# Tables of a state space layer made in the first stage, its work in other slots, and one root for the norm of all heads

## The reference

```python
z = rmsnorm(x, g_mix) @ w_in
q, k, v, u = split(z)                                # 1024 columns each
attn = diff_attend(rope(q), rope(k), v, ...)         # 8 heads; the 8 decoding tokens attend to 2048 cached ones each
o = o * rsqrt(mean(o * o, axis=-1) + EPS)            # norm of each head, over its 128 values
o = o * g_sub * (1.0 - lam_init)

# state space layer: 64 groups of 16 channels, 64 complex states each
dt = exp(log_dt); mag = exp(a_re * dt)
lr, li = mag * cos(a_im * dt), mag * sin(a_im * dt)
bbar = (lam - 1) / a * b                             # complex
h[t] = lam * h[t-1] + bbar @ u[t];  y = Re(c @ h) + d * u
y = gelu(y); y = y * sigmoid(y @ w_glu + b_glu)

x = x + concat(attn, y) @ w_out
x = x + peer(rmsnorm(x, g_ffn), ...)                 # product-key experts
y = rmsnorm(x, g_final)
```

## Time and profile before

| | |
|---|---|
| median of 3 runs | 3755.88 us (3750.92 to 3758.41) |
| profiled execution | 3757.6 us, its span 3755.8 |
| mean granted PE clock | 0.973 |
| busy: PE, DVE, ACT, POOL | 94%, 55%, 29%, 52% |
| HBM | 236 GB/s over the span |

### The profile page before, as it was taken

One profiled execution on the slowest core, in us unless ns is written; L12 is line 12 of the kernel. 1 busy time (PEld: TensorE's weight loads), 2 busy tenths in 40 slices (PEclk: granted clock), 3 DMA queues, 4 the chain that ended last, 5 costly groups with the idle time before them and its releaser, 6 DMA issues. The chain is left out here.

```text
span 3755.8 us, 57507 instructions
## 1 busy us (share of the span) xinstructions
PE 3526.1 (94%) x22816; PEld 3336.9 (89%) x22816; DVE 2071.7 (55%) x3748; ACT 1079.7 (29%) x1184; POOL 1944.8 (52%) x735
## 2 busy tenths in 40 slices
PE   8999966887997999999999999997999999999997
PEld 8988743556997999999999999997999999999997
DVE  4212076426103899974444444443677777767673
ACT  3111132235122222333333333332222222222222
POOL 3333217004434445666666566654766667767662
PEclk9999978898998999999999999998999999999999
DMA  5587676562321225777777777767877878778772
GB/s 217 197 298 289 238 209 222 183 233 108 115 110 73 79 98 180 281 272 275 276 290 274 275 276 289 285 265 277 299 280 289 303 291 295 288 296 296 294 286 102
DMA packets 252324, 892.41 MB, mean 238 GB/s; under 512 B 97873, under 2 KB 131154, under 8 KB 175058
## 3 DMA queue, kind: packets, MB, share of 16 engines
q1 hardware_dynamic: 168882, 548.78, 41.1%
q0 software_dynamic: 36864, 268.45, 17.5%
q10 hardware_dynamic: 46432, 73.32, 5.7%
HBM read 818.91 MB, written 69.21 MB: 236 GB/s over the span
## 5 line engine op out<-in xcount | busy, mean ns | idle before, releaser
L113 POOL TENSOR_TENSOR wl<-raw,wh 128x2048 fp32r<-128x2048 f32 x324 | 1525.0, 4707 | 1559.0 <-ACT wh L109 1558.9
L109 ACT ACTIVATE wh<-raw 128x2048 fp32r<-128x2048 f32 x324 | 620.4, 1915 | 2063.0 <-PE acc L1362 712.7
L1697 PE MATMUL acc<-vh,wh 128*128 128x392 f32 x2048 | 704.6, 344 | 43.1 <-DVE xt L1762 22.2
L1360 PE MATMUL acc<-hh,wh 128*128 128x392 f32 x2048 | 709.6, 346 | 5.8 <-POOL wl L113 5.8
L1361 PE MATMUL acc<-hl,wh 128*128 128x392 f32 x2048 | 698.3, 341 | 0.0
L1698 PE MATMUL acc<-vl,wh 128*128 128x392 f32 x2048 | 697.2, 340 | 0.0
L1699 PE MATMUL acc<-vh,wl 128*128 128x392 f32 x2048 | 696.2, 340 | 0.0
L1362 PE MATMUL acc<-hh,wl 128*128 128x392 f32 x2048 | 696.0, 340 | 0.0
L128 PE MATMUL acc<-hh,wh 128*128 128x256 f32 (+1 forms) x1952 | 557.3, 286 | 0.8 <-POOL wl L113 0.8
L129 PE MATMUL acc<-hl,wh 128*128 128x256 f32 (+1 forms) x1952 | 551.9, 283 | 0.0
L130 PE MATMUL acc<-hh,wl 128*128 128x256 f32 (+1 forms) x1952 | 550.4, 282 | 0.0
(11 more groups left out here) (323 smaller groups left out, 3914.7 us busy)
## 6 DMA issues: line engine op xcount, KB each, us to landing
raw<-units SPq DMA_DIRECT2D x324, 1024.0 KB, 4.9
kr<-cache_k SPq DMA_DIRECT2D x128, 512.0 KB, 5.7
vr<-cache_v SPq DMA_DIRECT2D x128, 512.0 KB, 5.6
expert_acts<-ast ACTq DMA_DIRECT2D x128, 196.0 KB
expert_gates<-gs ACTq DMA_DIRECT2D x14, 1792.0 KB, 6.4
a<-expert_acts SPq DMA_DIRECT2D x32, 784.0 KB
g<-expert_gates SPq DMA_DIRECT2D x32, 784.0 KB
xt<-x_t SPq DMA_DIRECT2D x4, 1040.0 KB, 12.5
```

The costliest lines, as they stand in the source:

```text
L109: act.activation(m.wh[s][:, :, :], m.raw[s][:, :, :], ACT.Copy).then_inc(m.hi_done, 1)
L113: pool.tensor_tensor(m.wl[s][:, :, :], m.raw[s][:, :, :], m.wh[s][:, :, :].bitcast(F32), ALU.subtract).then_inc(m.lo_done, 1)
L1360: pe.matmul(o, m.wh[s][:, k, :], m.hh[:, k, NA:T], start=(k == 0), stop=False)
L1697: pe.matmul(o, m.wh[s][:, 4 * e + d, :], vh[gg][:, e, :], start=(e == 0), stop=False)
```

## The change

Three things.

1. The tables move into stage one. DVE makes angles after its cosine and sine tables, powers, input matrix and step tables after the first pair of q units, and the input steps of the four quarters around the next pairs. ACT does their exponentials and sines before its loop over units. `bb`, `pc`, `npc`, `a1`, `a2` stay in SBUF; input steps and output steps (made in units 24 to 29, in 16 halves) are stored to HBM (`eD`, `qD`) and loaded back by SP in the merged stage. The key chunks begin at unit 10, not 8. The channel inputs are stored with their 8 steps reversed, by 18 DVE instructions in place of 4, and loaded in four transfers of 128 rows in place of 8 of 16 rows.

2. In the merged stage DVE makes no tables. Rows, shift, fix, Y and turn lie in other slots, and SP's loads of tables and inputs stand between those of pages. The low parts of the first two gate units are made by DVE in eight pieces in slots 44 to 47.

3. In `stage_d` PE sums head h into row h of one accumulator (`to_row`), ACT takes two roots of 8 rows, DVE one reciprocal, and PE spreads each row over 128 rows again (`from_row`), from where DVE multiplies. The low parts of the heads are made by DVE.

```diff
+C0 = 10
+
 def chunks_by(t):
-    return min(NCK, max(0, (t - N_Q + 1) * NCK // (N_IN - N_Q)))
+    return min(NCK, max(0, (t - C0 + 1) * NCK // (N_IN - C0)))
+
+FIRST_CHUNKS = (6, 8, 8)
+E_AFTER = {4: (0,), 5: (1,), 6: (2,), 7: (3,)}
+QQ_STEPS = ((0, 3), (3, 6), (6, 9), (9, 12), (12, 14), (14, 16), (16, 16), (16, 16))
...
 (stage_a, ACT, before its loop over units)
+            act.wait_ge(Z["params_in"], 48)
+            act.activation(f(3), f(2), ACT.Exp).then_inc(Z["exps_ready"], 1)
+            act.wait_ge(Z["exponents_ready"], 1)
+            act.activation(f(6), f(4), ACT.Exp).then_inc(Z["exps_ready"], 1)
+            act.wait_ge(Z["angles_ready"], 1)
+            act.activation(f(9), f(7), ACT.Sin).then_inc(Z["sines_ready"], 1)
+            act.activation(f(10), f(8), ACT.Sin).then_inc(Z["sines_ready"], 1)
...
 (stage_a, DVE)
+            exponents()
+            rope(0, m.qs)
+            all_powers()
+            input_matrix()
+            step_matrices()
+            rope(2, m.qs, lambda: input_steps(0))
+            input_steps(1)
+            rope(4, m.qs, lambda: input_steps(2))
+            input_steps(3)
+            rope(6, m.qs)
...
             for t in range(U_V, N_IN):
                 plain(t, False)
+                for k in range(*QQ_STEPS[t - U_V]):
+                    output_steps(k)
...
-QQ_MADE = {7: (0, 0), 8: (0, 1), 9: (1, 0), 10: (1, 1), 22: (2, 0), 23: (2, 1), 25: (3, 0), 26: (3, 1)}
-ROWS_SLOT = {10: 0, 14: 1, 26: 2, 33: 3}
-SHIFT_SLOT = {12: 0, 16: 1, 28: 2, 35: 3}
-FIX_SLOT = {18: (1, 2), 19: (3, 4)}
-Y_SLOT = {21: 0, 24: 1, 31: 2, 38: 3}
-TURN_SLOT = {22: 0, 25: 1, 32: 2, 39: 3}
+ROWS_SLOT = {7: 0, 11: 1, 27: 2, 30: 3}
+SHIFT_SLOT = {9: 0, 13: 1, 29: 2, 32: 3}
+FIX_SLOT = {20: (1, 2), 21: (3, 4)}
+Y_SLOT = {23: 0, 25: 1, 31: 2, 35: 3}
+TURN_SLOT = {24: 0, 26: 1, 32: 2, 36: 3}
...
-GLU_SPLIT = {45: N_IN, 46: N_IN + 1}
+GLU_SPLIT = {43: N_IN, 44: N_IN + 1}
+GLU_REST = {44: ((N_IN, 0), (N_IN, 1)), 45: ((N_IN, 2), (N_IN, 3)), 46: ((N_IN + 1, 0), (N_IN + 1, 1)), 47: ((N_IN + 1, 2), (N_IN + 1, 3))}
...
 (stage_m, SP, after the first six pages)
+            load_inputs(0)
+            load_input_steps(0)
             for i in range(VR, NPG * NS):
                 load_page(i)
+                if i == 6:
+                    load_inputs(1)
+                    load_input_steps(1)
+                if i == 8:
+                    load_inputs(2)
+                    load_inputs(3)
+                if i == 10:
...  initial states, d_t
+                    load_output_steps(0)
+                if i == 12:
+                    load_output_steps(1)
+                if i == 16:
+                    load_input_steps(2)
+                if i == 20:
+                    load_input_steps(3)
+                if i == 70:
+                    load_output_steps(2)
+                if i == 76:
+                    load_output_steps(3)
...
-HEADS_SCALED = ((0, 1), (2, 3, 4), (5, 6, 7), ())
-HEADS_SPLIT = ((0,), (1, 2, 3), (4, 5, 6), (7,))
+HEADS_SPREAD = {(1, 2): (0,), (1, 3): (1,), (2, 0): (2,), (2, 1): (3,), (2, 2): (4,), (2, 3): (5,), (3, 0): (6,), (3, 1): (7,)}
+HEADS_SPLIT = ((), (0, 1), (2, 3, 4, 5), (6, 7))
...
 (stage_d, PE)
+            def sum_head(h):
+                pe.wait_ge(S["head_squared"], h + 1)
+                for hf, (c0, n) in enumerate(HALVES):
+                    mm = pe.matmul(m.aux[0:H, hf, 0:n], to_row[:, h, :], sq[:, h % 4, c0:c0 + n], start=(h == 0), stop=(h == H - 1), skip_group_check=True)
+                mm.then_inc(S["head_summed"], 1)
+
+            def spread_head(h):
+                pe.wait_ge(S["root_inverse"], 1)
+                if h >= 2:
+                    pe.wait_ge(S["head_scaled"], 2 * (h - 1))
+                for hf, (c0, n) in enumerate(HALVES):
+                    mm = pe.matmul(m.aux[:, 2 * ((h + 1) % 2) + hf, 0:n], from_row[:, h, :], rs[:, c0:c0 + n], start=True, stop=True)
+                mm.then_inc(S["head_spread"], 1)
```

More of the change, by code:

```diff
@@ new lines, in stage_a @@
+    spare = m.top
+    zu = [at(f"zu{j}", [P, CL, NCH + 2 * NS]) for j in range(2)]
+    zo += [at(f"zo{2 + j}", [P, T], off=spare + j * CL * (NCH + 2 * NS) * 4) for j in range(2)]
+    work = spare - 6 * T * 4
+    cc = at("cc", [P, 2, GP, CH], off=work); qo = [at(f"qo{j}", [P, PPQ // 2, 9, CH], off=work + 4096 + j * 2304) for j in range(2)]; qt = at("qt", [P, PPQ // 2, 9, CH], off=work + 4096 + 2 * 2304)
+    assert m.end <= spare
+    qz = at("qz", [P, 8, NS, 32])
+    lamv = at("lamv", [P, 4, 64]); lamp = at("lamp", [P, 2, 64])
@@ new lines, in stage_a @@
+    kr = [at(f"kr{j}", [P, CHP, 8, P], F32, off=m.x0 + (j - 1) * CHP * 4096 if j else None) for j in range(RING)]
+    assert m.x0 + 2 * CHP * 4096 <= m.x0 + KT * T * 4 and m.top <= m.keep0, (m.top, m.keep0)
+    top, m.top = m.top, m.x0
+    s5sm = at("s5sm", [P, 24, GP]); bc = at("bc", [P, 2, GP, CH]); tr = at("tr", [P, GP * CH]); tr2 = at("tr2", [P, PPQ, CL, CH])
+    eb = [at(f"eb{j}", [P, 2, PPQ, CL, CH]) for j in range(2)]
+    assert m.top <= m.x0 + KT * T * 4
+    m.top = top
+    pw, npw, bb, pc, npc, a1, a2 = m.pw, m.npw, m.bb, m.pc, m.npc, m.a1, m.a2
@@ new lines, in stage_a @@
+    f = lambda j: s5sm[:, j, :]
+    coeffs = lambda x, g0, ng, n: x[:, g0:g0 + ng, :].unsqueeze(2).broadcast_to([P, ng, n, CH])
+    spread = lambda x, g0, ng, n: x[:, 0:n, g0:g0 + ng].rearrange("p j g -> p g j").unsqueeze(3).broadcast_to([P, ng, n, CH])
+    Z = {n: sem("z_" + n) for n in "params_in bc_in cc_in exps_ready exponents_ready angles_ready sines_ready powers_ready input_ready steps_ready e_made qq_made chain".split()}
+    e_stored, qq_stored = [sem(f"z_e{j}") for j in range(2)], [sem(f"z_q{j}") for j in range(2)]
@@ L250, in _ @@
                 act.wait_ge(st_z[z], 16 * (8 if z < 2 else 4 * 8 + 4))
+            for j in range(2):
+                act.wait_ge(e_stored[j], 16 * 4)
+                act.wait_ge(qq_stored[j], 16 * 8)
         @block.gpsimd
@@ new lines, in step_matrices @@
+            def step_matrices():
+                for r in range(2):
+                    ch(dve.tensor_copy(a1[:, r, :], pw[:, 0, 1, :]))
+                    ch(dve.tensor_copy(pc[:, r, 1, :], pw[:, r, CL, :]))
+                ts(a2[:, 0, :], pw[:, 1, 1, :], -1.0, None, ALU.mult)
+                ch(dve.tensor_copy(a2[:, 1, :], pw[:, 1, 1, :]))
+                ch(powers(pc, 1, 1, 1))
+                ch(powers(pc, 1, 2, 2))
+                ch(powers(pc, 1, 4, 4))
+                ts(npc[:, 1:SB + 1, :], pc[:, 1, 1:SB + 1, :], -1.0, None, ALU.mult)
+                dve.sem_inc(Z["steps_ready"], 1)
+                ts(npw[:, :, :], pw[:, 1, :, :], -1.0, None, ALU.mult)
@@ L547, in _ @@
             x.then_inc(S["samples_done"], 1)
-            for u in range(U_GLU, U_GLU + 2):
-                split_lo(m, pool, u, u % 2)
         @block.scalar
@@ L1020, in _ @@
                 split_lo(m, pool, U_GLU + n + 2, n % 2)
-                for h in HEADS_SPLIT[n]:
-                    head_low(h)
             with pool.Fori(0, N_OUT // 2) as i:
```

410 lines of the change are left out of this document (214 added, 196 removed).

## The result

The changed kernel takes 3767.68 us (median of 5 runs, 3761.47 to 3773.0), the kernel before 3755.88; the ratio is 1.0033 (95% interval 1.0022 to 1.0045). So it is slower by 12 us, small but clear of the noise, where I had forecast 12 faster.

The account below looks back on a forecast made before the run. PE was taken as the bound in stage one, the merged stage and the gate-and-heads stretch, so any PE gap costs time. Terms 41 - 8 - 34 - 4 - 7 = -12 gave 3744 us from 3755.9, range 3712 to 3774.

Parts of the forecast that it names:

- Together 277. -34.: Merged stage, heads 1 to 7: counted at 277 us against 311.4 before, a gain of 34 us.
- The lower bound, -18: Heads 1 to 7: gain if only output-step products in heads 1 and 2 and a third of the others were exposed.
- Stage one, +41: Stage one: added tables, DVE waits for POOL splits, low clock and key chunks cost 41 us (+7 to +60).
- hidden: Stage one, units with output steps: DVE's 11.8 us of work fits in a 13.5 us unit, costing PE nothing.
- The key chunks, +3: Stage one: 32 key chunks on 22 units, not 24, barely fit the transfers; 3 us (0 to 15).
- Head 0, -8: Merged stage, head 0: DVE table work goes, loads take its place; ends at 542, not 550.6 (-20 to +5).
- The seam, -4: Merged stage to gate: of PE's 6.9 us wait behind POOL's two splits, 4 us goes (0 to 6).
- The norm, -7: Gate and heads' norm: 78 us in place of 85.4, fewer reciprocals and roots, spreads added on PE; gain 7 us.
- B: Rival, stage one: DVE's small table instructions slip between POOL's, so it loses only 4.4 + 3; 3710 us, 12%.
- C: Rival, merged stage: pages bound it, every head gives its gain back as a wait of L735; 3778 us, 13%.
- D: Rival, stage one: key chunks come late, 1 to 1.5 us in each of 22 units; 3774 us, 8%.
- E: Rival, whole kernel: terms off by some us in both ways, so nothing is left; 3748 to 3764 us, 12%.

Follow-up runs that it names:

- the run with the slots of before: Kernel with third output-step buffer, spread tables, newly chosen slots and last gate unit reordered, but state work in the slots of before: 3710.8 us.
- the runs above: Kernel with third buffer, spread tables, reordered last gate unit: 3708.9 us with newly chosen slots, 3710.8 with those of before, 3724.8 with those of the change.
- the chosen ones: Slots rows 7, 14, 26, 30, shift 10, 16, 28, 34, Y 23, 25, 31, 37, turn 24, 26, 32, 38; alone on the changed kernel 3757.9 us.
- the run of stage one with both: Changed kernel with tables spread over stage one, third output-step buffer, and step tables between the reads of units 4 and 5: 3726.9 us.
- the last pair: Kernel with third buffer, spread tables and reordered last gate unit, in slots of before (3710.8 us) and in slots of the change (3724.8 us).
- the run with other slots: Changed kernel with only slots changed: rows 7, 14, 26, 30, shift 10, 16, 28, 34, Y and turn of the last quarter 37, 38: 3757.9 us.

## Why the prediction was wrong

**The step that failed: "Together 277. -34."** Heads 1 to 7 took 292.9 us. I had built the 277 up from 27 us a head plus the blocks plus a list of waits, and set it against a measured 311.4 (309.9 up to the last matmul, which is 1.5 of the 17 already). Whatever the list lacks is then booked as gain. It put the new slots at nothing, and they brought the waits for the shift (9.9 and 4.8 us; I had passed over "SHIFT_SLOT ... 29" and "ROWS_SLOT ... 30" as a move at no cost). It had 5 us for pages where PE waited 13.2. It had nothing for the clock, at which PE's busy time alone moved by 13.0. These are more than the 16 by which the count was short, since some of the pages and of the clock are in my 27 us a head, too; how they split is not shown. The lower bound, -18, is near the measured -17.0 and the 17.8 of the run with the slots of before, but that is luck in part: by its own words (the four products of heads 1 and 2 and a third of the other four, 6.04 us each) it comes to 32. The slots were shown to be a loss by the runs above (14 to 16 us in the medians), and no choice of slots here went below 288.1, so even the best was -21.8 in the profile, not -34.

**Stage one, +41: near in size, in part by luck.** The terms were off by -7, +4, -3 and +9. The stalls by the exclusion, its order and its places were as forecast (29.1 us of waits in units 1 to 8 against 36; only the first was released by POOL's low part and not by DVE), and the low clock took about 6 where I had 2 (units 0 to 8 took 139.1 us, nine of 11.5 are 103.5, and PE waited 29.1 of the difference). The sentence that failed is that the output steps are "hidden": I had counted DVE's busy time in a unit, 11.8 us, and not its wait for a store to land. It cost 8.5 us by the run with a third buffer. The key chunks, +3, cost nothing: no wait of PE for `kr` is in the trace. The run with the tables in pieces shows what I had not seen at all: none of the loss belonged to the idea. With no more than some 7 us of tables ahead of any read, and the step tables no longer between a rotation and a read, stage one is as short as before.

**Head 0, -8: gained 14.4.** The transfers ran at 338 GB/s with a share of 0.90, as I had taken from the earlier trace rows. PE's wait for pages fell from 19.3 to 10.0 us, that for the turned input steps (`et`) from 5.4 to 0.7; its busy time stayed at 54. What put my estimate 6 us too low is not shown.

**The seam, -4: right** (-4.7). PE started the gate 2.23 us after its last matmul.

**The norm, -7: -2.0.** Again an absolute count (78 us of 85.4) in place of a difference. The kernel before, counted in the same way, comes to 57.5 + 7.7 + 14.5 + 2 = 81.7, so 3.7 us of the 7 were in the way of counting. The spreads were mis-sized by little (9.1 against 7.6).

**The rivals.** B, that DVE slips between, is out: 4.58 us for 0.20. The trace of before had spoken against it, too. The pair at 58.02 that I gave as its evidence was under way when POOL's split came, so that POOL waited (5.17 us in place of 4.62), and the copy behind the pair then waited for that split, as DVE's and POOL's rows show:

```profile
59.36 4.46 DVE L332 COPY qs<-zo 128x8 f32<-128x8 f32 x1
```

```profile
58.63 5.17 POOL L113 TENSOR_TENSOR wl<-raw,wh 128x2048 fp32r<-128x2048 f32 x1 [7.26 <-ACT wh L109]
```

C, that pages bound the merged stage, is not what happened, though heads 1 to 7 gave less than the 22 us that I had named as its sign: the page block (L735, now L911) waits 13.2 us in 17 pieces, none over 2.1, where it waited 11.8 in 14 before, and these heads moved 229 GB/s. D didn't come: there is no wait for `kr`, and in PE's gaps of units 25 to 31 the transfers ran at 414 to 419 GB/s, above the bound that I had named with it (with 391, had shown this before). Nearest is E, terms off, but its terms were to cancel; they were off by +17, +5, +4 and -6.

**What stays open.** By the medians the slots of the change cost 14 to 16 us; the profiles of the same pairs account for 3 to 7 of it. Heads 1 to 7 differ from profile to profile with the same slots: 291.9 to 299.3 us in seven profiles with those of the change, 288.1 to 291.0 in three with the chosen ones, so the difference can be 11 us. The gap in the last rows block differs, too (6.2 us in the run of stage one with both, 9.05 in the changed kernel, 12.9 with the third buffer). So a longer wait in the four slower runs of the last pair would fit, but none of those four has a profile. Why the same shift takes so different a time to land is open. So is what gave heads 1 to 7 the better clock; as far as one profile tells, 8 of the 13 us are not the slots', since the run with the slots of before has 235.8 us of busy time there, where the kernel before has 243.8.

## What to carry to other kernels

Make every term a difference between two timelines, not an absolute count against a measured window: what the count forgets turns into gain. When work is moved to an engine with spare time, ask how much of it stands ahead of the one instruction that PE waits for; 54 us of tables cost 35 us in bunches and nothing in pieces of up to 7 us. What else stands there counts, too: the 7 us of step tables still cost 8.9 between a rotation and a read, and nothing behind the read. And list for each moved step the single buffers it shares: two steps that were five slots apart and are now one apart have a wait between them, though neither was changed.

## What the runs showed of the hardware

DVE and POOL took turns by whole instructions in both directions: with pieces of a quarter, DVE's products waited about 1 us each, and POOL's work of 4.6 us took 8.0. The Trainium skill has both directions ("SBUF — State Buffer", section "Who interferes with whom": the one that comes second waits for the other's whole instruction), and these runs agree. Copies and products with a constant waited as well (4.46 and 4.47 us above).

Eight transfers of 16 to 128 KB, in runs of 64 to 512 bytes, took ACT 6.1 us to issue in the run with the later rows block. They were issued from the smallest to the largest, and landed 3.0 to 13.1 us after their issue, while pages of 512 KB in the same stretch took 7.3. In the same place of the run with other slots, the largest took 4.8. So size alone was no guide to when a transfer lands. (My expectation of that run calls the one of 13.1 us the first; it was the last.)

The stores of output steps, 288 KB each, landed 4.6 to 8.6 us after their issue in the stretch where DVE waited for them.
